# Attention heads of the second block in pairs: eleven slots in place of twenty-two

## The chip, the cores and the metric

One core of a Trainium2 chip runs the whole program. The metric is the time of one execution on the device in microseconds (us); lower is better. The times of before are the median, lowest and highest of three runs. The engines are PE (TensorE: weight loads and matmuls), DVE (VectorE), ACT (ScalarE), POOL (GpSimd) and SP (SyncE, which issues most DMAs).

## What is computed

Two blocks over 256 tokens of width 1024. The first has an mLSTM layer and an HGRN2 layer with feed-forward parts. The second has three attention branches next to each other; only its attention is touched by the change. Its core, with 8 heads of 64 ("moba"), 8 heads of 64 ("fox") and 4 heads of 128 ("mem"):

```python
# moba and fox: causal, key <= query; fox adds cq - ck of a running sum to the scores
s = einsum('bhqd,bhkd->bhqk', q, k) * scale          # 256 x 256 per head
p = softmax(where(causal, s, -inf))
y = einsum('bhqk,bhkd->bhqd', p, v)
# mem: not causal, keys and values from `mem`
merged = (sigmoid(a_m) * (merge(y_m) @ w_br_moba)
          + sigmoid(a_f) * (merge(y_f) @ w_br_fox)
          + sigmoid(a_c) * (merge(y_c) @ w_br_mem))
x = x + merged @ w_out
```

With 256 tokens there is one moba block, so moba is plain causal attention. The gates a_m, a_f, a_c are 1024 wide each: products of the normed input with parts of w_in.

## The kernel before

Each engine has its own instruction stream, written out by hand; semaphores tie them together. Weight matrices stream from memory in units of 128x2048 fp32: SP fetches one into raw, ACT rounds it to whi (L626), DVE makes the rest wlo = raw - whi (L1882), and PE takes three products for each (L1172 to L1174, `three`). There are three buffers whi/wlo, and two units are prepared ahead. A unit is used in two halves: `stream_half(u, i)` takes the 12 products of 128x512 of the token tile i.

The attention of the 20 heads (16 of 64, 4 of 128) is woven into the streaming of 18 such units, ATT_UNITS: 12 for the gates (four for each branch) and 6 for the branches' output matrices. Before the change the weaving goes by slots of one head. In slot g PE does

- `scores(g)`: for each tile of 128 queries a product q k^T of 128 keys (tile 0, causal) or 256 keys, out of the rows 64 (h % 2) to 64 (h % 2) + 63 of `acc` for heads of 64 (L1753), a product for the fox term (L1755), and for causal heads the mask as a 128x128 bf16 product (L1757). The plain products are fp32 and appear in the trace as two passes each, a LDWEIGHTS and a MATMUL for every pass.
- a half of a unit; then `prob_transposes(g - 1)` (L1770, three or four of 128x128); in the first two slots a second half;
- `head_values(g - 2)`: p v for head g - 2, columns of 64 (L1785, 256 columns of p moving, and L1787, 128 of them for causal heads), written to the partitions 0 to 63 or 64 to 127 of bank 4 or 5.

The scores of even heads go to PSUM bank 0 and those of odd heads to bank 2, the transposed probabilities to banks 1 and 3. The streamed gate products go to banks 6 and 7.

DVE in the same slot: `normalise_probs(g - 1)` (L2839 to L2841), `score_max(g)` (L2859 to L2861), where an output of 128 columns is complete `split_values` (L2870, L2871), `lo` for the unit to come (L1882), `copy_probs(g - 1)` (L2849). ACT: `hi` for the unit to come (L626), `exponential(g)` (L1125), and, after the last half of a gate, `gate` (L1134), which frees banks 6 and 7 for the next one. SP only fetches weights.

The wait that starts the stage is that for the last normed queries and keys (L2815). After the 20 heads PE goes on with the six units of the output matrices, and what follows (w_out, the last feed-forward part) is streamed products again.

Of the kernel before, what the change touches and what calls it, by code (L numbers as in the profile page):

```python
# [92 lines left out]
def branch_units(b):  # L93
# [3 lines left out]

ATT_UNITS = (gate_units(0) + gate_units(1) + gate_units(2)
             + branch_units(0) + branch_units(1) + branch_units(2))
ATT_HALVES = (2, 2) + (1,) * 20  # L100
ATT_SLOTS = len(ATT_HALVES)
ATT_INSIDE = sum(ATT_HALVES) // 2
assert ATT_SLOTS == N_HEADS + 2 and len(ATT_UNITS) == ATT_INSIDE + 6


def att_halves(slot):

    done = sum(ATT_HALVES[:slot])
    return [divmod(x, 2) for x in range(done, done + ATT_HALVES[slot])]


def starts_first(slot):

    return [u for n, (u, i) in enumerate(att_halves(slot)) if i == 0 and n == 0]


def starts_later(slot):

    return [u for n, (u, i) in enumerate(att_halves(slot)) if i == 0 and n]


def att_bank(u):
# [32 lines left out]
def t_bank_s(gh):  # L155

    return 2 * (gh % 2)


def t_bank_o(n):  # L160

    return 4 + n % 2
# [60 lines left out]
def build(nc, t, out):  # L223
# [4 lines left out]
    with ctx:  # L228
# [226 lines left out]
        def at_least(eng, s, v):  # L455

            if not isinstance(v, int) or v > 0:
                eng.wait_ge(s, v)
# [136 lines left out]
        def _(act):  # L595
# [32 lines left out]
            def his(w, k):  # L628
                for _ in range(k):
                    hi(w)  # L630
# [486 lines left out]
            def exponential(gh):  # L1117

                _, _, dh, causal, _ = BRANCHES[HEAD_OF[gh][0]]
                act.wait_ge(t_max, gh + 1)  # L1120
                at_least(act, t_tp, gh - 1)
                bank = t_bank_s(gh)
                n0 = 128 if causal else 256
                for k, (c0, n) in enumerate(((0, n0), (n0, 256))):
                    ins = act.activation(prb[:, gh % 2, c0:c0 + n], ps[:, bank, c0:c0 + n], ACT.Exp,  # L1125
                                         bias=nmx[:, 2 * (gh % 2) + k:2 * (gh % 2) + k + 1], scale=dh ** -0.5,
                                         accum_out=rsum[:, 2 * (gh % 2) + k:2 * (gh % 2) + k + 1])
                ins.then_inc(t_exp, 1)

            def gate(u):  # L1130

                _, b, c, _ = ATT_UNITS[u]
                act.wait_ge(w_used, first_unit + u + 1)
                act.activation(gate_at[b][c], ps[:, att_bank(u):att_bank(u) + 2, :], ACT.Tanh, scale=0.5)\  # L1134
                   .then_inc(g_tanh, 1)
                act.wait_ge(g_tanh, 2 * b + c + 1)
                act.sem_inc(ps_free, 1)

            for slot in range(ATT_SLOTS):
                his(w, len(starts_first(slot)))  # L1140
                if slot < N_HEADS:
                    exponential(slot)
                for u, i in att_halves(slot):
                    if i == 1 and ATT_UNITS[u][0] == "g" and ATT_UNITS[u][3] == 4:
                        gate(u)
                his(w, len(starts_later(slot)))
            his(w, len(ATT_UNITS) - ATT_INSIDE)
            second_half(factor=0.5)
            his(w, 4)
# [10 lines left out]
        def _(pe):  # L1160
# [575 lines left out]
            pe.wait_ge(fox_set, 1)  # L1736
            pe.wait_ge(ps_free, w.pair)

            def scores(gh):

                b, h = HEAD_OF[gh]
                _, _, dh, causal, fox = BRANCHES[b]
                per = 128 // dh
                qT = acc[:, b, 0:1024].rearrange("p (k t) -> p k t", k=4)
                kT = acc[:, b, 1024:2048].rearrange("p (k t) -> p k t", k=4)
                n0 = 128 if causal else 256
                at_least(pe, t_exp, gh - 1)
                bank = t_bank_s(gh)
                ro, kt = dh * (h % per), h // per
                q, k = qT[ro:ro + dh, kt, :], kT[ro:ro + dh, kt, :]  # L1750
                for i, (c0, n) in enumerate(((0, n0), (n0, 256))):
                    o = ps[:, bank, c0:c0 + n]
                    ins = pe.matmul(o, q[:, 128 * i:128 * (i + 1)], k[:, 0:n], start=True, stop=not causal)  # L1753
                    if fox:
                        pe.matmul(o, fox_l[:, h, 128 * i:128 * (i + 1)], fox_r[:, 0:n], start=False, stop=False)  # L1755
                    if causal:
                        ins = pe.matmul(ps[:, bank, c0 + n - 128:c0 + n], identb[:, :], maskb[:, 0, :],  # L1757
                                        start=False, stop=True)
                ins.then_inc(t_s, 1)

            def prob_transposes(gh):

# [7 lines left out]
                    ins = pe.transpose(ps[:, bank, c_out:c_out + 128], p[:, c_in:c_in + 128], ident)  # L1770
                ins.then_inc(t_tp, 1)

            def head_values(gh):

                b, h = HEAD_OF[gh]
                _, _, dh, causal, _ = BRANCHES[b]
                ro = dh * (h % (128 // dh))
                bank = t_bank_o(OUT_OF[gh])
                if ro == 0:
                    at_least(pe, t_y, OUT_OF[gh] - 1)  # L1780
                pe.wait_ge(t_pt, gh + 1)
                p = pts[:, gh % 2, :]
                v = mkv[:, 1] if b == 2 else qkv[:, 3 * b + 2]
                q0 = 128 if causal else 0
                pe.matmul(ps[ro:ro + dh, bank, 0:256], v[:, 0, dh * h:dh * (h + 1)], p[:, 0:256],  # L1785
                          start=True, stop=False)
                pe.matmul(ps[ro:ro + dh, bank, q0:256], v[:, 1, dh * h:dh * (h + 1)], p[:, 256:512 - q0],  # L1787
                          start=False, stop=True).then_inc(t_o, 1)

            unit_at = {}  # L1790

            def stream_half(u, i):

                kind, b, c, k0 = ATT_UNITS[u]
                if i == 0:
                    if kind == "b":
                        pe.wait_ge(t_y, 4 * b + 4)
                    if k0 == 0:
                        p, _ = w.next_pair()
                        pe.wait_ge(ps_free, p if u < ATT_INSIDE else p - 2)  # L1800
                    n, unit_at[u] = w.next_unit()
                    pe.wait_ge(w_lo, n + 1)
                wh = whi[:, unit_at[u], :].rearrange("p (k n) -> p k n", k=4)
                wl = wlo[:, unit_at[u], :].rearrange("p (k n) -> p k n", k=4)
                sh, sl, s0, kts = (AH, AL, k0, KT) if kind == "g" else (HH, HL, 4 * b, 4)
                for k in range(4):
                    ins = three(ps[:, att_bank(u) + i, :], sh[:, s0 + k, 128 * i:128 * (i + 1)],
                                sl[:, s0 + k, 128 * i:128 * (i + 1)], wh[:, k, :], wl[:, k, :],
                                k0 + k == 0, k0 + k == kts - 1)
                if i == 1:  # L1810
                    ins.then_inc(w_used, 1)

            for slot in range(ATT_SLOTS):
                halves = att_halves(slot)
                if slot < N_HEADS:
                    scores(slot)
                stream_half(*halves[0])
                if 1 <= slot <= N_HEADS:
                    prob_transposes(slot - 1)
                for half_ in halves[1:]:  # L1820
                    stream_half(*half_)
                if slot >= 2:
                    head_values(slot - 2)
            for u in range(ATT_INSIDE, len(ATT_UNITS)):
                for i in range(TT):
                    stream_half(u, i)
# [23 lines left out]
        def _(dve):  # L1850
# [34 lines left out]
            def los(w, k):  # L1885
                for _ in range(k):
                    lo(w)
# [976 lines left out]
            def split_values(gh):  # L2864

                n = OUT_LAST[gh]
                dve.wait_ge(t_o, gh + 1)
                bank = t_bank_o(n)
                hh, hl = HH[:, n, :], HL[:, n, :]
                link(dve.tensor_copy(hh, ps[:, bank, 0:SEQ]))  # L2870
                dve.tensor_tensor(hl, ps[:, bank, 0:SEQ], hh.bitcast(fp), ALU.subtract).then_inc(t_y, 1)  # L2871
# [18 lines left out]
                elif k0 == 4:  # L2890
                    w.next_pair()

            for slot in range(ATT_SLOTS):
                if 1 <= slot <= N_HEADS:
                    normalise_probs(slot - 1)
                if slot < N_HEADS:
                    score_max(slot)
                if slot - 3 in OUT_LAST:
                    split_values(slot - 3)
                los(w, len(starts_later(slot - 1)) if slot else 0)  # L2900
                los(w, len(starts_first(slot)))
                if 1 <= slot <= N_HEADS:
                    copy_probs(slot - 1)
                for u, i in att_halves(slot):
                    if i == 1:
                        finish(u)
            los(w, len(starts_later(ATT_SLOTS - 1)))
            split_values(N_HEADS - 1)
            for u in range(ATT_INSIDE, len(ATT_UNITS)):
                lo(w)  # L2910
                finish(u)
# [40 lines left out]
```

## Time and profile before

| | us |
|---|---|
| median of 3 runs | 1595.64 |
| lowest, highest | 1595.47, 1600.07 |
| the profiled execution | 1599.27 |
| its span | 1597.5 |

| engine | busy us in the span | share |
|---|---|---|
| PE | 1495.5 | 94% |
| PEld (weight loads) | 1285.0 | 80% |
| DVE | 1161.6 | 73% |
| ACT | 750.4 | 47% |

The span runs from the first to the last instruction. PE matmuls are pipelined: the duration of one is longer than what it adds to the time, so the distance between starts is what counts. PEclk is the granted clock of TensorE as a share of 2.4 GHz.

### The profile page before, as it was taken

How to read it: one execution, taken by the hardware profiler on the slowest of the kernel's cores; microseconds unless marked ns; L12 is line 12 of the kernel's file. 1: busy time of each engine (PE TensorE's matmuls, PEld its weight loads, DVE VectorE, ACT ScalarE, POOL GpSimd, SP SyncE). 2: the span in 40 equal slices, each digit the busy share in tenths (PEclk: the TensorE clock that was granted, in tenths of full speed). 3: DMA queues.
4: the chain of work that ended last, by engine and by line, in shares of the span. 5: the costliest groups of instructions: out<-in, count | busy, mean ns of one | idle time of the engine just before them, and what ended most of it. 6: DMA issues, size and time to landing. Idle time of an engine off the chain costs nothing. (4 is left out here: it accounts for less than half of the span.)

```text
span 1597.5 us, 20884 instructions
## 1 busy us (share of the span) xinstructions
PE 1495.5 (94%) x8256; PEld 1285.0 (80%) x8256; DVE 1161.6 (73%) x1231; ACT 750.4 (47%) x757; POOL 7.7 (0%) x9
## 2 busy tenths in 40 slices
PE   3998899999699998999999999989899999999997
PEld 2876799898698877887888788867776778799996
DVE  5788876676678764988889888876985567555554
ACT  1534243333362633677767676744343333343331
POOL 0000000000000000000000000000000000000000
PEclk9998999999899997999999999999999999999999
DMA  9776556967464561998998999943353234445642
GB/s 307 252 280 246 186 196 220 319 226 244 164 211 159 185 210 35 343 332 302 345 347 305 330 318 350 319 133 131 126 190 102 84 103 161 132 135 171 209 151 98
DMA packets 197113, 345.73 MB, mean 216 GB/s; under 512 B 11601, under 2 KB 90033, under 8 KB 190897
## 3 DMA queue, kind: packets, MB, share of 16 engines
q1 hardware_dynamic: 189280, 339.76, 62.6%
q10 hardware_dynamic: 7760, 4.97, 1.1%
q8 instruction: 51, 0.84, 0.2%
q14 instruction: 22, 0.17, 0.0%
HBM read 343.65 MB, written 1.05 MB: 216 GB/s over the span
## 5 line engine op out<-in xcount | busy, mean ns | idle before, releaser
L1882 DVE TENSOR_TENSOR wlo<-raw,whi 128x2048 fp32r<-128x2048 f32 (+2 forms) x220 | 480.0, 2193 | 159.4 <-ACT whi L626 155.4
L626 ACT ACTIVATE whi<-raw 128x2048 fp32r<-128x2048 f32 (+2 forms) x220 | 402.8, 1836 | 354.7 <-PE ps L1174 242.6
L1172 PE MATMUL ps<-whi,AH 128*128 128x512 f32 (+1 forms) x816 | 324.8, 398 | 18.3 <-DVE wlo L1882 9.6
L1174 PE MATMUL ps<-whi,AL 128*128 128x512 f32 (+1 forms) x816 | 314.0, 385 | 0.0
L1173 PE MATMUL ps<-wlo,AH 128*128 128x512 f32 (+1 forms) x816 | 313.7, 384 | 0.0
L1172 PE MATMUL ps<-AH,whi 128*128 128x256 f32 x896 | 255.7, 285 | 3.6 <-DVEq L1934 1.5
L1173 PE MATMUL ps<-AL,whi 128*128 128x256 f32 x896 | 254.4, 284 | 0.0
L1174 PE MATMUL ps<-AH,wlo 128*128 128x256 f32 x896 | 254.3, 284 | 0.0
L1172 PEld LDWEIGHTS ps<-whi,AH 128*128 128x128 f32 x816 | 155.1, 190 | 59.9 <-DVE wlo L1882 17.2
L1174 PEld LDWEIGHTS ps<-whi,AL 128*128 128x128 f32 x816 | 154.7, 190 | 28.6
L1172 PEld LDWEIGHTS ps<-AH,whi 128*128 128x128 f32 x896 | 172.9, 193 | 5.7 <-issue 3.4
L1173 PEld LDWEIGHTS ps<-wlo,AH 128*128 128x128 f32 x816 | 155.3, 190 | 25.3 <-issue 0.2
L1173 PEld LDWEIGHTS ps<-AL,whi 128*128 128x128 f32 x896 | 172.9, 193 | 0.0
L1174 PEld LDWEIGHTS ps<-AH,wlo 128*128 128x128 f32 x896 | 172.9, 193 | 0.0
L1172 PE MATMUL ps<-whi,HH 128*128 128x512 f32 x432 | 170.9, 396 | 0.2 <-DVE wlo L1882 0.2
L1174 PE MATMUL ps<-whi,HL 128*128 128x512 f32 x432 | 168.3, 390 | 0.0
L1173 PE MATMUL ps<-wlo,HH 128*128 128x512 f32 x432 | 168.3, 390 | 0.0
L1882 DVE TENSOR_TENSOR wlo<-acc,whi 128x2048 fp32r<-128x2048 f32 (+1 forms) x48 | 101.1, 2113 | 22.6 <-ACT whi L626 21.8
L626 ACT ACTIVATE whi<-acc 128x2048 fp32r<-128x2048 f32 (+1 forms) x48 | 85.1, 1772 | 32.1 <-PE ps L1174 32.1
L1172 PEld LDWEIGHTS ps<-whi,HH 128*128 128x128 f32 x432 | 81.1, 188 | 19.4 <-DVE wlo L1882 2.2
L1174 PEld LDWEIGHTS ps<-whi,HL 128*128 128x128 f32 x432 | 81.1, 188 | 17.2
L1173 PEld LDWEIGHTS ps<-wlo,HH 128*128 128x128 f32 x432 | 81.2, 188 | 16.1 <-issue 0.2
(314 smaller groups left out, 1583.3 us busy)
## 6 DMA issues: line engine op xcount, KB each, us to landing
raw<-in_ada_w SPq DMA_DIRECT2D x48, 1024.0 KB, 5.5
raw<-in_w_in SPq DMA_DIRECT2D x26, 1024.0 KB, 5.2
raw<-in_moe_w_up SPq DMA_DIRECT2D x24, 1024.0 KB, 7.2
raw<-in_h_w_in SPq DMA_DIRECT2D x16, 1024.0 KB, 5.8
raw<-in_moe_w_gate SPq DMA_DIRECT2D x16, 1024.0 KB, 7.2
raw<-in_moe_w_down SPq DMA_DIRECT2D x16, 1024.0 KB, 6.2
acc<-in_moe_w_down SPq DMA_DIRECT2D x16, 1024.0 KB, 7.7
raw<-in_m_w_in SPq DMA_DIRECT2D x12, 1024.0 KB, 6.1
```

What stands on the lines that cost most here:

```text
L626: act.activation(whi[:, h, 0:n], raw_at[s][:, 0:n], ACT.Copy).then_inc(w_hi, 1)
L1172: pe.matmul(o, sh, mh, start=first, stop=False)
L1173: pe.matmul(o, sh, ml, start=False, stop=False)
L1174: return pe.matmul(o, sl, mh, start=False, stop=last)
L1882: dve.tensor_tensor(wlo[:, h, 0:n], raw_at[s][:, 0:n], whi[:, h, 0:n].bitcast(fp), ALU.subtract)\
```

## The change

The slots go by pairs (2n, 2n+1) of heads: ten slots with a pair's scores and one behind. In `scores(n)` the products of the even head (rows 0 to 63) and of the odd head (rows 64 to 127) stand next to each other for each query tile, then the fox terms of both, then the masks of both. In `head_values(n)` the products of the even head (columns to partitions 0 to 63) and of the odd head (64 to 127) stand next to each other. Heads of 128 go in pairs in the same code. In a slot PE now does the scores of pair s, the transposes of pair s - 1, half a unit, the values of pair s - 1, the other half (slot 0 has four halves; the last slot has half, transposes, half, values). Values come one slot behind the scores, not two. DVE does `score_max` of both, `copy_probs` of both of the last pair, `lo`, `normalise_probs` of both, `split_values` of the last pair. ACT does `hi`, then the exponentials of both, then a gate where one is complete. No arithmetic is added or left out.

```diff
@@ -97,26 +97,10 @@
...
              + branch_units(0) + branch_units(1) + branch_units(2))
-ATT_HALVES = (2, 2) + (1,) * 20
-ATT_SLOTS = len(ATT_HALVES)
-ATT_INSIDE = sum(ATT_HALVES) // 2
-assert ATT_SLOTS == N_HEADS + 2 and len(ATT_UNITS) == ATT_INSIDE + 6
-def att_halves(slot):
-    done = sum(ATT_HALVES[:slot])
-    return [divmod(x, 2) for x in range(done, done + ATT_HALVES[slot])]
-def starts_first(slot):
-    return [u for n, (u, i) in enumerate(att_halves(slot)) if i == 0 and n == 0]
-def starts_later(slot):
-    return [u for n, (u, i) in enumerate(att_halves(slot)) if i == 0 and n]
+N_PAIRS = N_HEADS // 2
+ATT_UNITS_IN = ((0, 1),) + tuple((u,) for u in range(2, 12))
+ATT_INSIDE = 12
+assert len(ATT_UNITS_IN) == N_PAIRS + 1 and len(ATT_UNITS) == ATT_INSIDE + 6
 def att_bank(u):
@@ -1136,14 +1120,14 @@
...
                 act.sem_inc(ps_free, 1)
-            for slot in range(ATT_SLOTS):
-                his(w, len(starts_first(slot)))
-                if slot < N_HEADS:
-                    exponential(slot)
-                for u, i in att_halves(slot):
-                    if i == 1 and ATT_UNITS[u][0] == "g" and ATT_UNITS[u][3] == 4:
-                        gate(u)
-                his(w, len(starts_later(slot)))
+            for slot, units in enumerate(ATT_UNITS_IN):
+                hi(w)
+                if slot < N_PAIRS:
+                    exponential(2 * slot)
+                    exponential(2 * slot + 1)
+                his(w, len(units) - 1)
+                if ATT_UNITS[units[-1]][3] == 4:
+                    gate(units[-1])
             his(w, len(ATT_UNITS) - ATT_INSIDE)
...
@@ -1736,27 +1720,34 @@
...
             pe.wait_ge(ps_free, w.pair)
-            def scores(gh):
-                b, h = HEAD_OF[gh]
+            def scores(n):
+                pair_ = (2 * n, 2 * n + 1)
+                b, _ = HEAD_OF[2 * n]
                 _, _, dh, causal, fox = BRANCHES[b]
...
                 n0 = 128 if causal else 256
-                at_least(pe, t_exp, gh - 1)
-                bank = t_bank_s(gh)
-                ro, kt = dh * (h % per), h // per
-                q, k = qT[ro:ro + dh, kt, :], kT[ro:ro + dh, kt, :]
-                for i, (c0, n) in enumerate(((0, n0), (n0, 256))):
-                    o = ps[:, bank, c0:c0 + n]
-                    ins = pe.matmul(o, q[:, 128 * i:128 * (i + 1)], k[:, 0:n], start=True, stop=not causal)
-                    if fox:
-                        pe.matmul(o, fox_l[:, h, 128 * i:128 * (i + 1)], fox_r[:, 0:n], start=False, stop=False)
-                    if causal:
-                        ins = pe.matmul(ps[:, bank, c0 + n - 128:c0 + n], identb[:, :], maskb[:, 0, :],
-                                        start=False, stop=True)
-                ins.then_inc(t_s, 1)
+                at_least(pe, t_exp, 2 * n)
+                for i, (c0, width) in enumerate(((0, n0), (n0, 256))):
+                    for gh in pair_:
+                        h = HEAD_OF[gh][1]
+                        ro, kt = dh * (h % per), h // per
+                        q, k = qT[ro:ro + dh, kt, :], kT[ro:ro + dh, kt, :]
+                        ins = pe.matmul(ps[:, t_bank_s(gh), c0:c0 + width], q[:, 128 * i:128 * (i + 1)], k[:, 0:width],
+                                        start=True, stop=not causal)
+                        if i and not causal:
+                            ins.then_inc(t_s, 1)
+                    for gh in pair_:
+                        o = ps[:, t_bank_s(gh), c0:c0 + width]
+                        if fox:
+                            pe.matmul(o, fox_l[:, HEAD_OF[gh][1], 128 * i:128 * (i + 1)], fox_r[:, 0:width],
+                                      start=False, stop=False)
+                        if causal:
+                            ins = pe.matmul(o[:, width - 128:width], identb[:, :], maskb[:, 0, :], start=False, stop=True)
+                            if i:
+                                ins.then_inc(t_s, 1)
             def prob_transposes(gh):
@@ -1770,22 +1761,25 @@
...
                 ins.then_inc(t_tp, 1)
-            def head_values(gh):
-                b, h = HEAD_OF[gh]
+            def head_values(n):
+                pair_ = (2 * n, 2 * n + 1)
+                b, _ = HEAD_OF[2 * n]
                 _, _, dh, causal, _ = BRANCHES[b]
-                ro = dh * (h % (128 // dh))
-                bank = t_bank_o(OUT_OF[gh])
-                if ro == 0:
-                    at_least(pe, t_y, OUT_OF[gh] - 1)
-                pe.wait_ge(t_pt, gh + 1)
-                p = pts[:, gh % 2, :]
                 v = mkv[:, 1] if b == 2 else qkv[:, 3 * b + 2]
                 q0 = 128 if causal else 0
-                pe.matmul(ps[ro:ro + dh, bank, 0:256], v[:, 0, dh * h:dh * (h + 1)], p[:, 0:256],
-                          start=True, stop=False)
-                pe.matmul(ps[ro:ro + dh, bank, q0:256], v[:, 1, dh * h:dh * (h + 1)], p[:, 256:512 - q0],
-                          start=False, stop=True).then_inc(t_o, 1)
+                at_least(pe, t_y, OUT_OF[2 * n + 1] - 1)
+                pe.wait_ge(t_pt, 2 * n + 2)
+                for i in range(TT):
+                    for gh in pair_:
+                        h = HEAD_OF[gh][1]
+                        ro = dh * (h % (128 // dh))
+                        c0 = q0 if i else 0
+                        ins = pe.matmul(ps[ro:ro + dh, t_bank_o(OUT_OF[gh]), c0:256], v[:, i, dh * h:dh * (h + 1)],
+                                        pts[:, gh % 2, 256:512 - q0] if i else pts[:, gh % 2, 0:256],
+                                        start=i == 0, stop=i == 1)
+                        if i:
+                            ins.then_inc(t_o, 1)
             unit_at = {}
@@ -1810,17 +1804,24 @@
...
                     ins.then_inc(w_used, 1)
-            for slot in range(ATT_SLOTS):
-                halves = att_halves(slot)
-                if slot < N_HEADS:
+            for slot, units in enumerate(ATT_UNITS_IN):
+                last = slot == N_PAIRS
+                if not last:
                     scores(slot)
-                stream_half(*halves[0])
-                if 1 <= slot <= N_HEADS:
-                    prob_transposes(slot - 1)
-                for half_ in halves[1:]:
-                    stream_half(*half_)
-                if slot >= 2:
-                    head_values(slot - 2)
+                    if slot:
+                        prob_transposes(2 * slot - 2)
+                        prob_transposes(2 * slot - 1)
+                for u in units[:-1]:
+                    stream_half(u, 0)
+                    stream_half(u, 1)
+                stream_half(units[-1], 0)
+                if last:
+                    prob_transposes(2 * slot - 2)
+                    prob_transposes(2 * slot - 1)
+                elif slot:
+                    head_values(slot - 1)
+                stream_half(units[-1], 1)
+            head_values(N_PAIRS - 1)
             for u in range(ATT_INSIDE, len(ATT_UNITS)):
...
@@ -2890,22 +2891,32 @@
...
                     w.next_pair()
-            for slot in range(ATT_SLOTS):
-                if 1 <= slot <= N_HEADS:
-                    normalise_probs(slot - 1)
-                if slot < N_HEADS:
-                    score_max(slot)
-                if slot - 3 in OUT_LAST:
-                    split_values(slot - 3)
-                los(w, len(starts_later(slot - 1)) if slot else 0)
-                los(w, len(starts_first(slot)))
-                if 1 <= slot <= N_HEADS:
-                    copy_probs(slot - 1)
-                for u, i in att_halves(slot):
-                    if i == 1:
-                        finish(u)
-            los(w, len(starts_later(ATT_SLOTS - 1)))
-            split_values(N_HEADS - 1)
+            def finish_pair(n):
+                for gh in (2 * n, 2 * n + 1):
+                    if gh in OUT_LAST:
+                        split_values(gh)
+            for slot, units in enumerate(ATT_UNITS_IN):
+                if slot < N_PAIRS:
+                    score_max(2 * slot)
+                    score_max(2 * slot + 1)
+                if 0 < slot < N_PAIRS:
+                    copy_probs(2 * slot - 2)
+                    copy_probs(2 * slot - 1)
+                lo(w)
+                if slot < N_PAIRS:
+                    normalise_probs(2 * slot)
+                    normalise_probs(2 * slot + 1)
+                    if slot:
+                        finish_pair(slot - 1)
+                else:
+                    copy_probs(2 * slot - 2)
+                    copy_probs(2 * slot - 1)
+                los(w, len(units) - 1)
+                for u in units:
+                    finish(u)
+            finish_pair(N_PAIRS - 1)
             for u in range(ATT_INSIDE, len(ATT_UNITS)):
...
```

## Rows read from the trace of the kernel before

**Rows 1.** Stages: window, us, busy (instructions) PE, PEld, DVE, ACT, POOL, PEclk, DMA, GB/s.

```profile
1200.80:1326.60 125.80, 125.73 (x578) 92.40 (x579) 74.47 (x175) 45.69 (x97) 0.00 (x0) 0.97 0.32 100
1326.60:1593.00 266.40, 258.00 (x1650) 234.97 (x1648) 148.66 (x126) 94.34 (x74) 1.81 (x1) 1.00 0.47 150
```

**Rows 2.** Waits from 1200.8 us: PE to 1360, DVE to 1330; us, times, longest.

```profile
PE ps L1753 <- DVEq L2815: 1.5, 1, 1.5
...
DVE col L2859 <- PE ps L1757: 25.3, 15, 5.7
```

**Rows 3.** PE timeline, a moba head: start us, us, what (passes merged), [idle before].

```profile
1238.00 0.49 PE L1770 MATMUL ps<-cst,Z 128*128 128x128 f32 x3
1238.41 0.65 PE L1785 MATMUL ps<-GB,Z 128*64 128x256 f32 x2
1238.90 0.38 PE L1787 MATMUL ps<-GB,Z 128*64 128x128 f32 x2
1239.21 0.48 PE L1753 MATMUL ps<-acc 64*128 64x128 f32 x2
1239.63 0.23 PE L1757 MATMUL ps<-maskb,identb 128*128 128x128 bf16 x1
1239.79 0.70 PE L1753 MATMUL ps<-acc 64*128 64x256 f32 x2
1240.41 0.23 PE L1757 MATMUL ps<-maskb,identb 128*128 128x128 bf16 x1
...
1240.77 0.40 PE L1173 MATMUL ps<-wlo,AH 128*128 128x512 f32 x1
```

**Rows 4.** PE timeline, the scores of a fox head and the stream behind.

```profile
1249.77 0.48 PE L1753 MATMUL ps<-acc 64*128 64x128 f32 x2
1250.18 0.49 PE L1755 MATMUL ps<-GB,AF 128*128 128x128 f32 x2
1250.51 0.22 PE L1757 MATMUL ps<-maskb,identb 128*128 128x128 bf16 x1
1250.66 0.70 PE L1753 MATMUL ps<-acc 64*128 64x256 f32 x2
1251.28 0.70 PE L1755 MATMUL ps<-GB,AF 128*128 128x256 f32 x2
1251.82 0.22 PE L1757 MATMUL ps<-maskb,identb 128*128 128x128 bf16 x1
...
1252.16 0.39 PE L1173 MATMUL ps<-wlo,AH 128*128 128x512 f32 x1
```

**Rows 5.** PE timeline, a mem head and stream products, all full tiles of 128*128.

```profile
1312.24 0.39 PE L1174 MATMUL ps<-whi,AL 128*128 128x512 f32 x1
1312.47 0.60 PE L1770 MATMUL ps<-cst,Z 128*128 128x128 f32 x4
1312.90 0.60 PE L1785 MATMUL ps<-GB,Z 128*128 128x256 f32 x2
...
1313.77 1.03 PE L1753 MATMUL ps<-acc 128*128 128x256 f32 x4
```

**Rows 6.** DVE timeline behind the scores of the moba head of rows 3.

```profile
1240.68 0.29 DVE L2859 TENSOR_REDUCE col<-ps 128x1 f32<-128x128 f32 x1 [0.94 <-PE ps L1757]
...
1241.41 0.42 DVE L2870 CAST HH<-ps 128x256 fp32r<-128x256 f32 x1
...
1242.21 2.28 DVE L1882 TENSOR_TENSOR wlo<-raw,whi 128x2048 fp32r<-128x2048 f32 x1
1244.41 0.55 DVE L2849 COPY GB<-ps 128x384 f32<-128x384 f32 x1
```

**Rows 7.** PE by stage: window, us, busy (instructions), PEclk, DMA share, GB/s.

```profile
1201.30:1208.10 6.80, 6.80 (x18) 0.50 0.13 21
```

**Rows 8.** PE timeline where full tiles of 128*128 follow a form of 128*64.

```profile
1298.47 0.38 PE L1787 MATMUL ps<-GB,Z 128*64 128x128 f32 x2
1298.78 0.92 PE L1753 MATMUL ps<-acc 128*128 128x256 f32 x3
```

## Prediction

> **What bounds the kernel now.** First the windows by stage. From the first score to the last value product the stage takes 125.8 us, of which PE is busy in 125.73, and behind it, to the last of the PE work, in 258.00 of 266.40 [rows 1]. Then the waits: PE waits once, 1.5 us for the last keys before the stage, and never inside it, while DVE waits 15 times, 25.3 us together, for PE's masks [rows 2]. So PE's queue sets the time here and 10 us of shorter PE work come out at the end nearly whole; DVE and ACT are done with room. A busy PE says nothing of what it does, so the timeline comes last, read by distances between starts. Where all tiles are full and nothing changes form, a pass of 512 columns adds 0.23 us, four passes of 128 add 0.43 (0.107 each), four of 256 add 0.87 (0.215 each) [rows 5]. That is the yardstick for what follows.
>
> In a moba head [rows 3] the three transposes from 1238.00 end by that yardstick at 1238.32, but the values start at 1238.41: a gap of 0.09. Their passes (two of 256, two of 128) are worth 0.645, and the scores start 0.80 after: 0.06 for the first weight load, which nothing covers, and again 0.09 of gap. The scores' first two passes of 128 take 0.42 to the mask for 0.215 of columns: 0.11 of load and 0.09 of gap. Mask to the next scores 0.16; two passes of 256 take 0.62 for 0.43; from the mask to the stream's first product 0.13 (its second stands at 1240.77, less 0.23). Each of the gaps stands where the form changes (128x64, 64x128, 128x128), none where it stays. So a moba head costs 0.09 + 0.42 + 0.16 + 0.62 + 0.13 = 1.42 for its scores and 0.09 + 0.06 + 0.645 = 0.80 for its values beside its transposes and stream. A fox head [rows 4] has 0.09 + 0.41 + 0.33 + 0.15 + 0.62 + 0.54 + 0.11 = 2.25 for its scores. These are five changes of form a head, for all 16 heads of 64.
>
> **The change, part by part.** (1) Fewer changes of form. Per pair they are: to the scores, to the masks or fox terms, back, and again to the full form, then to the values and back to the stream: six in place of ten. Counted as if the two heads' passes still ran one after the other: moba scores 0.09 + (0.42 + 0.215) + (0.16 + 0.06) + (0.62 + 0.43) + (0.13 + 0.06) = 2.19, where the second mask is not shown alone and I take 0.06 (0.053 for 128 columns at the pace of the stream up to 0.10 for the recorded load). Before: 2.84. Saved 0.65. Fox: 0.09 + 0.41 + 0.215 + 0.33 + 0.215 + 0.21 + 0.62 + 0.43 + 0.54 + 0.43 + 0.17 = 3.66 where 4.50 were: 0.84. The values lose a little: one gap and one short load in front in place of two, but now the stream stands behind them, which costs a gap and a full load. Such a return is seen once: after the last passes of 128x64, worth 0.215 from 1298.47, the full tiles come at 1298.78, a gap of 0.09 [rows 8], and then a load of 0.11 [rows 3]. So 0.09 + 0.06 + 1.29 + 0.20 = 1.64 where 1.60 were: 0.04 lost. Sum: 4 x (0.61 + 0.80) = 5.6 us. Heads of 128 have no change of form and gain nothing.
>
> (2) Passes next to each other. The order in a pair is even 1, even 2, odd 1, odd 2. An odd product uses other rows (or other columns) of the array than the even one, so odd 1 can run beside even 2; odd 2 has to wait for odd 1 and even 2 for even 1. In the scores of the second tile that is one pass of 256, 0.215. In the first tile a pass (0.107) is as long as the load of its weights (0.11 [rows 3]), and four loads have to come one after the other, so I take nothing there. In the values the loads are short (0.06) and the chain goes on from part 0 to part 1: odd 1 beside even 2, then even's next pass of 128 beside odd 2; 1.29 become 0.86, 0.43 saved. Per pair 0.645, for 8 pairs 5.2 us. No row of before has two such products next to each other, so this is bounded from nothing to the whole half, below. "TensorE: Matmul & The Clock Gate" of the Trainium skill (Part 3, packing small matmuls) says that matmuls in different row or column groups start some 4 ns apart and that starts and ends keep program order; with it the sum holds as written, without it 5.2 us are missing. No run here shows it yet.
>
> (3) Waits. The values now come one slot behind the scores, so the chain scores, maxima, copies, values lies in one slot. Behind the last mask of a pair DVE needs 0.27 to start (1240.41 to 1240.68), 0.73 for each head's maximum (1240.68 to 1241.41), and two copies of 0.55 [rows 3, 6]: 0.27 + 1.46 + 1.10 = 2.83 to the second copy's end. PE meanwhile does the mask's rest 0.13, six transposes 0.64, half a unit 12 x 0.23 = 2.74 and a gap 0.09: 3.60. Room 0.8 us, in mem pairs the same (maxima 0.13 longer a head, transposes 0.22 longer in all). The transposes need the last slot's normalising, which is done in that slot's other half. DVE's whole slot is 1.46 + 1.1 + 2.2 (`lo`, 1242.21 to 1244.41) + 0.8 (split, 1241.41 to 1242.21) + the normalising of two heads, three short operations each like the maxima, so about 1.46 again: 7.0 us [rows 6], against PE's 2.19 + 1.64 + 0.64 + 5.5 - 0.645 = 9.3; ACT is busy 45.69 us of 125.80 [rows 1]. In the last slot `lo` stands ahead of the last two copies; there PE has two halves of 2.74 between. I cost the waits at nothing; with that cover gone each us of DVE's lateness beyond 0.8 is paid ten times. SP's queue: no fetch is added or moved past another, the DMA share is 0.32 [rows 1].
>
> (4) Start of the stage. The clock is at its lower level, 0.50, from 1201.3 to 1208.1 [rows 7], after PE's wait of 1.5 us and the short work ahead. Now the scores of two heads fall in it, not of one, and a longer part of it is 64-row work. If it rises at the same place, nothing changes.
>
> **The sum.** 5.6 + 5.2 = 10.8 us off the profiled execution, 1599.27: 1588.5. This execution is 3.6 us over the median of the runs, 1595.64; the same saving from the median gives 1584.9, my forecast, 0.68% faster. 0.3% (4.8 us) is about what a measurement here can tell from no change.
>
> **Rivals.** A, it doesn't do what it says: fp32 passes never run beside each other, and only the gaps go: 5.6 us, 1590.0. For: before has no such pair, and every product here is two passes in turn. Against: before changes rows and columns at every head, so nothing there could have shown it.
>
> B, only row groups overlap: the values of both heads go to one PSUM bank (4 or 5), the scores to two (0 and 2). If writes into one bank exclude each other, 8 x 0.43 = 3.4 us are missing: 1588.3. "TensorEngine Tiling (Array Packing)" of the Trainium skill (Restrictions and Gotchas) says of row tiles that they can't access the same bank at once; the values here are column tiles, of which it doesn't say so.
>
> C, whole overlap: both heads' passes run in twos throughout, the loads too. Then the first tile gives 0.215, the second another 0.215, the values another 0.215: 8 x 0.645 = 5.2 us more, 1579.7. "TensorEngine Tiling (Array Packing)" (Theoretical Speedup) gives up to 2x for a dimension of 64, which is this. Against it: even 2 can't start before even 1 ends.
>
> D, the clock: if the stretch at 0.50 becomes half as long again (3.4 us), half of that is lost, 1.7 us: 1586.6.
>
> E, the other side: DVE takes the place of PE as the bound. Its queue is in order, and `score_max` stands behind `lo` and the normalising of the slot before; `lo` waits for ACT's whi, which waits for the unit's last half and, every other slot, the gate. If DVE came to the maxima later by a `lo` (2.2) and one head's normalising (0.75, as above), the copies would end at 2.83 + 2.95 = 5.78 against PE's 3.60: 2.2 us in each of ten slots, 22 against 10.8: 1606.8. It decides from 0.8 + 10.8/10 = 1.9 us of lateness a slot. Against it: DVE's own waits for PE today are 25.3 us in 15 of 20 heads [rows 2].
>
> **How the numbers follow.** Forecast 0.52, A 0.18, B 0.10, C 0.08, D 0.06, E 0.06. Leaving out C and E's far ends, the range goes from 1581.5 (part of C, a second mask at no cost) to 1592.0 (A and D together, 1591.7). Faster by over 0.3% (under 1590.9): the forecast, B, C, D and two thirds of A, with some of the unseen, 0.82; within 0.3%: the rest of A and small lateness, 0.13; slower, E at its full size, 0.05.
>
> **What would show it.** In the timeline of PE: an odd score pass of 256 starting with the even head's second (both in one row or with starts 0.01 us apart), the second tile's four passes taking about 0.75 and not 0.96, the values' eight about 0.91 and not 1.34; gaps of 0.09 six times a pair; no row of waits of PE for DVE in the stage (E would put "PE <- DVE GB L2849" or its like there with over 10 us); PEclk back at 1.0 by about 7 us into the stage. The stage should shrink from 125.8 to about 115, and nothing behind it should change. The prediction is wrong if the stage shrinks and the time behind it grows, or if a wait appears in the stage.

## The result and the profile after

| | before | after |
|---|---|---|
| median (lowest to highest), us | 1595.56 (1588.2 to 1600.07), 4 runs | 1578.18 (1573.16 to 1581.01), 4 runs |
| profiled execution, us | 1599.27 | 1581.01 |
| first score to last value pass, us | 125.3 | 107.6 |
| from there to the end of the span, us | 271.35 | 271.29 |

The ratio is 0.9892, interval 0.9847 to 0.9937: 1.1% faster. In a second set of runs it was 1577.38 against 1597.22, ratio 0.9890, interval 0.9864 to 0.9915. The forecast, 1584.9, had the direction and the stage, and about 60% of the size; the time lies below its range, which began at 1581.5. No ratio counts one execution of 2459.86 us, of the slots alone below, whose granted clock was 0.56 where the others have 0.97 to 0.98.

The windows by stage of the kernel after, for the stage and for what follows (window, us, busy us and instructions of PE, PEld, DVE, ACT and POOL, PEclk, DMA share, GB/s):

```profile
1200.20:1308.20 108.00, 107.92 (x577) 81.79 (x578) 72.50 (x173) 44.86 (x98) 0.00 (x0) 0.98 0.36 114
1308.20:1575.00 266.80, 258.13 (x1651) 235.08 (x1649) 149.14 (x128) 93.79 (x73) 1.80 (x1) 1.00 0.47 151
```

They answer to [rows 1]. Nearly as many PE records are done in 17.8 us less, PE is busy as before, and the stretch behind is as long as it was: the second window is set by hand (266.80 here, 266.40 in [rows 1]); counted from the last value pass it is 271.3 us in both. The waits of PE in the stage and behind it, and those of DVE in the stage (us, times, longest):

```profile
PE ps L1738 <- DVEq L2816: 1.5, 1, 1.5
```

```profile
DVE col L2860 <- PE ps L1748: 22.3, 8, 3.5
DVE wlo L1883 <- ACT whi L610: 5.6, 3, 3.2
```

As in [rows 2], PE waits once, for the last keys, and DVE still waits for PE's masks; its waits for ACT's whi were 2.4 us in 2 times before. No new wait of PE has come. So the gain lies in what PE's own instructions cost. The timeline of PE, a moba pair, its values and the next pair (start us, us of the merged group, passes merged):

```profile
1222.94 0.49 PE L1738 MATMUL ps<-acc 64*128 64x128 f32 x4
1223.37 0.28 PE L1748 MATMUL ps<-maskb,identb 128*128 128x128 bf16 x2
1223.58 0.70 PE L1738 MATMUL ps<-acc 64*128 64x256 f32 x4
1224.22 0.28 PE L1748 MATMUL ps<-maskb,identb 128*128 128x128 bf16 x2
...
1227.83 0.87 PE L1778 MATMUL ps<-GB,Z 128*64 128x256 f32 x8
1228.63 0.50 PE L1156 MATMUL ps<-whi,AH 128*128 128x512 f32 x1
...
1231.62 0.38 PE L1738 MATMUL ps<-acc 64*128 64x128 f32 x2
```

Set beside [rows 3]: four passes of 128 take 0.43 to the mask where two took 0.42; four of 256 take 0.64 where two took 0.62; the eight value passes take 0.80 where four took 0.80. Two heads cost what one did, in the scores of both tiles and in the values. The forecast had 0.64, 1.05 less 0.215, and 1.01 (a load of 0.06, 0.86, a gap of 0.09) for these three. The fox pairs show the same, with the fox terms (full tiles) still one after the other. How the passes lie is seen in a short window of the score passes, in the kernel after (the first passes of the two heads, 128 columns each, start at 1222.942 and 1222.949) and in the kernel before:

```profile
1222.90:1223.05 0.15, 0.11 (x2) 1.00 0.95 369
```

```profile
1239.15:1239.30 0.15, 0.09 (x1) 1.00 0.00 0
```

(Window, us, busy us of PE with its passes of this line, PEclk, DMA share, GB/s.) The odd head's first pass runs beside the even head's first; the second passes follow at 1223.156 and 1223.162.

### The profile page after: what moved, and what is told of

Its sections match the earlier page's. It is cut to its first block and busy times, and to the rows that moved or that the text cites. A ratio compares the mean times of both kernels' runs of the same rounds, so it can differ in the third digit from the quotient of the medians.

```text
span 1579.2 us, 20882 instructions
## 1 busy us (share of the span) xinstructions
PE 1477.4 (94%) x8256; PEld 1272.5 (81%) x8256; DVE 1158.9 (73%) x1231; ACT 748.8 (47%) x757; POOL 7.7 (0%) x9
## 3 DMA queue, kind: packets, MB, share of 16 engines
HBM read 343.65 MB, written 1.05 MB: 218 GB/s over the span
## 5 line engine op out<-in xcount | busy, mean ns | idle before, releaser
L610 ACT ACTIVATE whi<-acc 128x2048 fp32r<-128x2048 f32 (+1 forms) x48 | 85.1, 1773 | 32.4 <-PE ps L1158 32.4
L1157 PEld LDWEIGHTS ps<-wlo,HH 128*128 128x128 f32 x432 | 81.2, 188 | 16.1 <-issue 0.2
```

The costliest lines, as they stand in the source:

```text
L610: act.activation(whi[:, h, 0:n], raw_at[s][:, 0:n], ACT.Copy).then_inc(w_hi, 1)
L1157: pe.matmul(o, sh, ml, start=False, stop=False)
```

## The experiments

Each stage time here is read in that run's own profile, from the first score to the last value pass. "Behind" it, all of them have 271.3 us.

**The kernel before again.** No edit.

> The kernel before, unchanged, profiled once more. The stage from the first score to the last value pass took 125.3 us in the first profile, of which 6.8 us of PE work lay at the lower clock from 1201.3. If that lower stretch belongs to the kernel (one head's scores at the start), it is 6.8 us again and the stage 125.3 again. If it hangs on where the clock's changes happen to fall, it can be 3.4 us, and the stage 123.6.

Measured: stage 125.26 again, 6.8 us of it at the lower clock again.

**The kernel after again.** No edit.

> The kernel after, unchanged. Stage 107.6 us in its first profile with a lower stretch of 3.4 us. If the short stretch comes from the paired scores at the start, 3.4 and 107.6 again; if it is chance, 6.8 and 109.3 are possible. Time against before: both theories 0.989 within 0.003 (17.3 us by the stage and the start).

Measured: stage 107.57, 3.4 us at the lower clock again, ratio 0.9890. Both kernels repeat to 0.05 us in the stage; the spread of the whole times, some 10 us, comes from earlier stages: in the 14 profiles the first score starts at 1192.5 to 1201.4 us, after 58 to 85 us at the lower clock. On the whole more of it goes with a later start, though not in every pair (85 us and 1200.9 before, 78 us and 1201.4 before again).

**The slots alone.** Scores and values in the old order within the pair (the edit in short):

```diff
-                for i, (c0, width) in enumerate(((0, n0), (n0, 256))):
-                    for gh in pair_:            # product of both, then masks of both
+                for gh in pair_:
+                    for i, (c0, width) in enumerate(((0, n0), (n0, 256))):
+                        # product, fox term, mask of one head and tile
...
-                for i in range(TT):
-                    for gh in pair_:
+                for gh in pair_:
+                    for i in range(TT):
```

> Eleven slots, all waits and the work of DVE and ACT as after, but on PE the products in the old order: the whole even head, then the whole odd head. Theory 1 (products beside each other bring the gain): only the merged slots are left, two changes of form a pair fewer and odd's first value pass beside even's last ones, about 0.2 to 0.4 us a pair, so 2 to 3 us faster than before, 15 us slower than after; the stage 122 to 124 us. Rival (the longer slots bring it): within 3 us of after, the stage under 111 us.

Measured: ratio 0.9975 (0.9954 to 0.9995), stage 119.4, between the two numbers for it (122 to 124, under 111), which was the surprise of this run: 5.9 us gained and not 2 to 3. The slots of two moba heads are 9.92 us, where two slots of before make 10.56. Nearly all of it is in the values, which with their gaps and loads take 1.00 us of the stream for a pair, where the forecast's reading of before has 1.60 for two heads. One pair's values in the timeline, then the passes of that line from 1221.640 to 1221.665, then those from 1221.6 to 1222.1, split by shape:

```profile
1221.65 0.88 PE L1773 MATMUL ps<-GB,Z 128*64 128x256 f32 x8
1222.45 0.50 PE L1156 MATMUL ps<-whi,AH 128*128 128x512 f32 x1
```

```profile
L1773 PE MATMUL ps<-GB,Z x2: 429/430/430, 1221.6 to 1221.7; 128*64 128x256 f32 x2
```

```profile
L1773 PE MATMUL ps<-GB,Z x4: 378/404/430, 1221.6 to 1221.9; 128*64 128x256 f32 x4
```

In this kernel the loop over the heads stands outside the one over the parts, so PE's instructions are even 256 columns, even 128, odd 256, odd 128. Each is one instruction in the program and two passes in the trace: the 20 heads issue 40 of them in line 1773, and the trace has 80 records:

```profile
L1773 PE MATMUL ps<-GB,Z x80: 272/378/431, 1221.6 to 1318.3; 128*64 128x256 f32 x32, 128*64 128x128 f32 x32, 128*128 128x256 f32 x16
```

The first four passes on the chip are all of 256 columns, two at a time (starts 1221.646 and 1221.659, 1221.913 and 1221.926), and the 128 columns come only from 1222.128 on. The records don't name the head; but the even head has only two passes of 256, so the other two are the odd head's, 13 ns behind and ahead of the even head's 128. So here a product started while an earlier one, which needed the busy half of the array, still waited.

**The same part of the array.**

```diff
-                        ro, kt = dh * (h % per), h // per
+                        ro, kt = 0, h // per
...
-                        ro = dh * (h % (128 // dh))
+                        ro = 0
```

(and the sum of both heads' values is one accumulation).

> The order of after, with as many changes of form, but the odd head of 64 takes the even head's rows in its scores and the even head's columns in its values, so both products need the same part of the array. Part of the computation is changed: the odd heads' scores are the even ones', and the values of both are summed into the even head's partitions. Theory 1 (a product's two passes stay with its part of the array, and two products run beside each other whole): every pair costs 0.107 x 2 + 0.215 x 2 + 0.645 = 1.29 us more than after, 10.3 us in all, stage 118 us, in the timeline the four score passes of 256 take 0.96 and the eight value passes 1.34. My forecast's order (half of it overlaps): 5.2 us more, stage 113 us. Rival (the gain lies in the changes of form alone): as after, 107.6 us.

Measured: ratio 0.9967 (0.9950 to 0.9984), stage 119.2. The timeline of PE, as above:

```profile
1211.87 0.71 PE L1738 MATMUL ps<-acc 64*128 64x128 f32 x4
1212.51 0.29 PE L1748 MATMUL ps<-maskb,identb 128*128 128x128 bf16 x2
1212.73 1.13 PE L1738 MATMUL ps<-acc 64*128 64x256 f32 x4
1213.79 0.29 PE L1748 MATMUL ps<-maskb,identb 128*128 128x128 bf16 x2
...
1217.43 1.51 PE L1778 MATMUL ps<-GB,Z 128*64 128x256 f32 x8
1218.88 0.50 PE L1156 MATMUL ps<-whi,AH 128*128 128x512 f32 x1
...
1221.82 0.37 PE L1738 MATMUL ps<-acc 64*128 64x128 f32 x1
```

Four passes of 128 now take 0.64, four of 256 take 1.06, the values 1.45: the same products in the same order with the overlap gone. In the values, the passes of 256 now start one by one, 0.215 us apart behind the first. A moba slot is 9.95 against 8.67, a fox slot 11.51 against 10.27: 1.28 and 1.24, where theory 1 said 1.29. The stage is 1.2 us over its 118; that is the clock, 6.8 us at its lower level and not 3.4, below.

**Scores paired, values in the old order.** The second half of the edit of the slots alone, that of the values.

> As after, but the values in the old order: both products of the even head, then both of the odd head. In the run with the slots alone the odd head's first value pass started 13 ns after the even head's first, ahead of the even head's second product, which stands before it in the program. Theory (products for different parts of the array start as soon as their part is free, whatever stands between): the eight value passes take 0.80 us as after and the stage 107.6 us. Rival (only neighbours in the program run beside each other): 0.2 us a pair more, stage 109.2 us.

Measured, in one execution: stage 107.85, the value passes 0.80, the slots 8.71 and 10.31 against 8.67 and 10.27. The theory holds: that even and odd values alternate in the program brings 0.04 us a pair; that they stand between the same two changes of form brings the rest.

**Masks last.** The products of both tiles first, then the fox terms and masks of both; `start` is set for a bank's first product alone (the edit in short):

```diff
-                for i, (c0, width) in enumerate(((0, n0), (n0, 256))):
-                    ... products of both heads, then fox and mask of both heads
+                for i, (c0, width) in tiles:
+                    ... products of both heads, start=i == 0
+                for gh in pair_:
+                    for i, (c0, width) in tiles:
+                        ... fox and mask, stop=i == 1
```

> As after, but within the scores of a pair the products of both query tiles come first and the fox terms and masks of both tiles behind them (the second tile's product no longer opens a group of its own), two changes of form a pair fewer. By the gap of 0.09 and the load of 0.11 at each: about 0.3 us less in each moba pair and 0.4 in each fox pair, 2.9 us in all, stage 104.7 us, time 0.987 to 0.988 of before. Rival (the maxima now start later and PE waits for DVE): the stage stays at 107 to 108 us and a wait of PE for DVE stands in it.

Measured: ratio 0.9888 (0.9869 to 0.9908), stage 105.2, slots 8.40 and 9.93: 0.27 and 0.34 less than after. Right in kind, a little under in size; no wait of PE.

**Masks last, values behind the slot's second half unit.**

```diff
-                elif slot:
-                    head_values(slot - 1)
                 stream_half(units[-1], 1)
-            head_values(N_PAIRS - 1)
+                if slot:
+                    head_values(slot - 1)
```

> As the kernel with the masks last, and the values of a pair behind the slot's second half unit, right ahead of the next pair's scores, in place of between the halves: the form goes from 128x64 to 64x128 directly, one return to full tiles (gap 0.09 and load 0.11) a slot fewer, 0.2 us in nine slots, 1.7 us. Stage 103.0 us, time 0.986 of before. Rival (DVE's split of the values comes too late for the next maxima): waits of PE in the stage and no gain over the masks alone.

Measured: ratio 0.9864 (0.9832 to 0.9895), stage 104.4, slots 8.12 and 9.67: 0.28 and 0.26 less than with the masks alone, where 0.2 was expected. The stage is 1.4 us over the expected 103.0: in this profile the clock fell 1.2 us ahead of the first score and stayed low for 6.8 us. It is the fastest by its median, 1576.47; in the whole times alone it can't be told from the kernel after, whose interval overlaps its own, while the stage shows the difference.

> Masks and values last, again: if the clock falls behind the first score, 3.4 us at the lower clock and a stage of 103.4 us (104.4 less the 1.0 us that its first profile lost by falling 1.2 us ahead); if it falls ahead, 104.4 us again.

Measured: stage 103.3, with 3.4 us at the lower clock: as expected. The timeline of PE where the values and the next pair's scores meet:

```profile
1217.46 0.87 PE L1780 MATMUL ps<-GB,Z 128*64 128x256 f32 x8
...
1218.26 0.93 PE L1739 MATMUL ps<-acc 64*128 64x128 f32 x8
1219.12 0.40 PE L1750 MATMUL ps<-maskb,identb 128*128 128x128 bf16 x4
1219.35 0.83 PE L1763 MATMUL ps<-cst,Z 128*128 128x128 f32 x6
```

The eight score passes and four masks of a pair take 1.09, where they take 1.40 in the kernel after (1222.94 to 1224.34).

**The first pair's scores one after the other, three times.**

```diff
-                        ro, kt = dh * (h % per), h // per
+                        ro, kt = dh * (h % per) if n else 0, h // per
```

> As after, but in the scores of the first pair alone the odd head takes the even head's rows, so the two products of each tile run one after the other there (that head's scores are then the even one's). Theory (the lower clock stretch at the start is 3.4 us and not 6.8 because the array is fuller in it): 6.8 us at the lower clock again, the first slot 13.95 + 1.7 and some 0.5 for its own passes, stage 109.7 us, about 2 us over after. Rival (where the change of clock falls is chance): 3.4 us, the first slot about 0.5 longer, stage 108.1 us.

> The kernel with the first pair's score products one after the other, profiled again: in its first profile the clock fell 1 us before the first score, not behind it as in all others but one, so it told nothing. If the clock falls within 0.5 us behind the first score this time: theory (a fuller array lets it rise sooner) 6.8 us at the lower clock, first slot 16.0; chance 3.4 us, first slot 14.3.

> The same again, as the place of the fall differs from run to run: 6.8 us and a first slot of 16.0 by the theory, 3.4 us and 14.3 by chance.

Measured: ratio of the first 0.9901 (0.9873 to 0.9929). Stages 109.4, 109.8, 109.7; the clock fell 1.0 us ahead of the first score in the first of them, 0.3 behind it and 0.2 ahead of it in the others. The lower stretch was 6.8 us each time. Windows of two such stretches, this kernel's second profile and the kernel after:

```profile
1197.24:1204.00 6.76, 6.76 (x20) 4.74 (x20) 3.60 (x7) 1.72 (x8) 0.00 (x0) 0.50 0.00 0
```

```profile
1200.44:1203.85 3.41, 3.41 (x15) 2.15 (x15) 1.10 (x5) 0.27 (x2) 0.00 (x0) 0.50 0.00 0
1203.90:1207.30 3.40, 3.40 (x16) 2.79 (x15) 3.29 (x8) 1.40 (x8) 0.00 (x0) 1.00 0.00 0
```

All other slots are those of the kernel after to 0.02 us; the first is 15.8, 16.2 and 16.1 in place of 13.97, of which some 1.7 is the clock.

**The slots alone again.**

> The slots alone, products in the old order, again: theory 6.8 us at the lower clock, stage 119.4; by chance 3.4 us and 117.7.

Measured: stage 120.9, 10.2 us at the lower clock. Neither number: longer still than the theory said. It is one execution.

Over all profiles, counted from the first score to the rise of the clock, where the fall lay within 0.5 us of that score:

| first pair's products | profiles | from the first score to the rise, us |
|---|---|---|
| beside each other | 5 (after twice, scores paired, masks last, masks and values last) | 3.2 to 3.9 |
| one after the other | 7 (before twice, slots alone twice, same part, first pair apart twice) | 6.6 to 7.3, once 10.1 |

In the two left over, one of each kind, the clock fell 1.0 and 1.2 us ahead, and rose after 5.6 and 5.9. A rival is when the full-tile stream starts: 2.1 to 2.3 us after the first score in the kernel after and with the scores paired, 1.8 to 2.0 with the masks last, but 3.3 to 4.4 in the slots alone, the same part and the first pair apart, so those runs don't separate it from the pairing. Only the two profiles of the kernel before speak against it: there it starts 1.8 us after the first score, and yet the clock rises after 7.1 and 7.3.

## Why the prediction was wrong in size

| term, us | forecast | measured | from |
|---|---|---|---|
| fewer changes of form | 5.6 | 5.4 | same part: slots 9.95 and 11.51 against two of 5.28 and 6.13, four pairs each |
| passes beside each other | 5.2 | 10.1 | after against same part: 1.28 and 1.24, four pairs each |
| the clock at the start | 0 | 1.7 | 3.4 us less at half rate |
| the rest of the stage | 0 | 0.4 | what is left of 125.3 - 107.6 = 17.7 |
| ahead of the stage | 0 | 0.6 | 1200.87 and 1200.28, the same program |

The measured column adds up to 18.2 of the 18.26 us between the two profiled executions.

Right: that PE's queue alone sets the stage and that all of its saving comes out at the end; that no wait takes its place (rival E: DVE had room in its chain and waits for PE's masks 22.3 us in 8 times; no variant has a wait of PE in the stage); the price of a change of form, term by term (1), within 0.2 us of 5.6; that heads of 128 gain nothing; and what rival A, no overlap at all, comes to: 119.7 us of stage by its sum (125.3 less 5.6), 119.2 in the run with the same part.

Wrong: step (2). "The order in a pair is even 1, even 2, odd 1, odd 2" took the passes to start strictly in this order, so that odd 1 waits until even 2 starts, and so it counted half of the overlap. The trace has even 1 with odd 1 and even 2 with odd 2, 6 or 7 ns apart. The two passes of an fp32 product are one instruction in the program, and in the slots alone a whole instruction was passed; either is enough to free odd 1, and no run tells which of the two did it in the kernel after. So the overlap is whole, 10.1 us where the sum has 5.2, and rival C, given 0.08 and 1579.7, is what happened (1578.18 measured, with the clock's 1.7 in it). The step's second half, that four loads of 0.11 have to come one after the other, fell too: the two heads' loads start in pairs (1222.941 and 1222.947, then 1223.049 and 1223.056, in the kernel after), and the tile of 128 columns costs 0.43 for two heads. The argument written against C, that even 2 can't start before even 1 ends, was true and beside the point. Of the Trainium skill, "TensorE: Matmul & The Clock Gate" (Part 3, packing small matmuls) has matmuls start in program order some 4 ns apart: the trace shows starts 6 or 7 ns apart, and in the slots alone 13, but there not program order, which is the part of the rule that I took into the sum. "TensorEngine Tiling (Array Packing)" (Theoretical Speedup), up to 2x for a dimension of 64, agrees with this trace: 1.06 us for four passes of 256 with their load and gap become 0.64. Rival B fell in the same rows: the values of both heads go to one bank and still take 0.80.

Step (4) took the clock as unchanged, and rival D had it going the other way. The sign was a matter of what the paired scores do to the lower stretch, and the rows of before, with one head's scores only, had no word on it.

The range was drawn around half the overlap. It began at 1581.5, above C's 1579.7, since C had so small a chance; had the question "is it one instruction or two" been left open, as it was, the range should have reached it. The chances have a slip too: the terms named for "faster by over 0.3%" add up to 0.88 (0.52, 0.10, 0.08, 0.06 and two thirds of 0.18), and the 0.82 doesn't follow from them.

What stays open: what in the paired scores lets the clock rise sooner. In 12 profiles, without an exception in either direction, it rose sooner where the two products ran beside each other, and it rose later again in the two telling profiles in which only the first pair was taken apart; two profiles don't tell. The runs don't separate how full the array is from how fast the products come, or, but for the kernel before, from when the stream starts. Why the slots alone once stayed low for 10.2 us is open too.

## What to carry to other kernels

Where TensorE sets the time and a product fills half the rows or columns, look for its counterpart on the other half and put both between the same two changes of form; here the paired products of two heads took what those of one had, and each change of form avoided gave 0.14 to 0.28 us (0.27 and 0.34 for two with the masks last, 0.28 and 0.26 for one with the values last). They need not stand next to each other in the program (tried with the values): what counts is that nothing of another form comes between. Ahead of a sum over queued passes, look in the program whether they are one instruction or several, and let the range reach the case that the order in the queue doesn't hold.

## What the runs showed of the hardware

- A matmul for free columns of the array started ahead of an earlier matmul in the program that needed busy ones (the slots alone): starts 1221.646 and 1221.659 for the two heads' 256 columns, with the even head's 128 between them in the program and only at 1222.128.
- Two column halves wrote one PSUM bank at the same time with no loss: 0.80 us for eight passes and for four.
- A change of form (128x128, 64x128, 128x64) cost about 0.09 us of gap and the load behind it, 0.05 (64 columns of weights) to 0.11 (128); the gap is 0.08 to 0.10 in the rows of before, after and the variants.
- With its first products paired, the stage left the lower clock 3.2 to 3.9 us after its first score, and 6.6 us or more with them in turn, where the clock had fallen within 0.5 us of that score (12 profiles).
